# A projection chunk of the hybrid trunk kernel: products with high weight halves first, then those with low halves

## The reference, cut to what matters

```
h    = rmsnorm(x, g_pre)
proj = einsum('bld,de->ble', h, w_in)      # even: 1024 x 5648, odd: 1024 x 4104
...                                        # gated MLP and SSD scan (even), forgetting attention (odd)
o    = einsum('ble,ed->bld', y, w_out)     # even: 2048 x 1024, odd: 1024 x 1024
x    = x + rmsnorm(o, g_post)
```

## Time and profile before

| | us |
|---|---|
| median of 3 runs | 1733.57 |
| lowest and highest | 1732.59, 1736.33 |
| span of the profiled execution | 1733.1 |
| PE busy in it | 1618.7 (93%) |
| DVE, ACT, POOL busy | 820.3, 639.0, 431.9 |
| granted TensorE clock, mean | 0.973 |

### The profile page before, as it was taken

One profiled execution on the slowest core, in us unless ns is written; L12 is line 12 of the kernel. 1 busy time (PEld: TensorE's weight loads), 2 busy tenths in 40 slices (PEclk: granted clock), 3 DMA queues, 4 the chain that ended last, 5 costly groups with the idle time before them and its releaser, 6 DMA issues.

```text
span 1733.1 us, 27903 instructions
## 1 busy us (share of the span) xinstructions
PE 1618.7 (93%) x10174; PEld 1529.1 (88%) x10174; DVE 820.3 (47%) x1738; ACT 639.0 (37%) x1146; POOL 431.9 (25%) x261
## 2 busy tenths in 40 slices
PE   5899999998998999899997899999999999997995
PEld 4899999988998999799995788889888888986894
DVE  5745776674883122711117833443434344344426
ACT  6433332332224222511123344444444444444213
POOL 1113443451212121512211321211212121124113
PEclk9999999999999999899998999999999999998997
DMA  4121222112102111111140235523232332201103
GB/s 140 39 64 55 67 82 67 54 42 78 45 19 61 37 42 43 37 37 48 46 120 9 37 64 49 68 43 67 42 65 49 46 67 43 67 31 50 32 18 100
DMA packets 150349, 93.97 MB, mean 54 GB/s; under 512 B 8994, under 2 KB 144836, under 8 KB 150300
## 3 DMA queue, kind: packets, MB, share of 16 engines
q1 hardware_dynamic: 150300, 93.30, 23.5%
HBM read 78.95 MB, written 14.34 MB: 54 GB/s over the span
## 4 chain that ended last, share of the span: by engine, by line
PE 77%; DVE 8%; ACT 6%; issue 5%; POOL 1%; DMA 1%; SPq 0%; POOLq 0%; ACTq 0%; DVEq 0%
PE PB L639 72%; PE PB L643 5%; DVE NRML L1462 2%; DVE HX L1469 1%; ACT HH L1086 1%; ACT L1092 1%; DVE HL L1462 1%; ACT SB L1418 1%; DVE O L1462 1%; DMA XS<-in_x_prompt_dram 1%; ACT L1349 1%; ACT NRMH L1086 0%; DMA nf_rows<-NFROW 0%; DVE O L1469 0%; POOL HL L617 0%
## 5 line engine op out<-in xcount | busy, mean ns | idle before, releaser
L639 PE MATMUL PB<-HH,WH 128*128 128x352 f32 x2256 | 752.0, 333 | 36.3 <-DVE HL L1462 11.5
L639 PE MATMUL PB<-HH,WL 128*128 128x352 f32 x2256 | 731.9, 324 | 0.0
L639 PE MATMUL PB<-HL,WH 128*128 128x352 f32 x2256 | 731.5, 324 | 0.0
L639 PEld LDWEIGHTS PB<-HH,WH 128*128 128x128 f32 x2256 | 429.9, 191 | 60.2 <-issue 39.8
L519 POOL TENSOR_TENSOR WL<-WRAW,WH 128x1024 fp32r<-128x1024 f32 x102 | 249.4, 2446 | 771.1 <-ACT WH L1086 771.1
L639 PEld LDWEIGHTS PB<-HL,WH 128*128 128x128 f32 x2256 | 431.3, 191 | 0.0
L639 PEld LDWEIGHTS PB<-HH,WL 128*128 128x128 f32 x2256 | 430.0, 191 | 0.0
L1086 ACT ACTIVATE WH<-WRAW 128x1024 fp32r<-128x1024 f32 x102 | 107.4, 1054 | 90.0 <-PE PB L639 70.6
L1462 DVE TENSOR_TENSOR TMP<-O 128x352 f32 x48 | 25.2, 525 | 199.7 <-ACT O L1106 199.3
L1418 ACT ACTIVATE SB<-SB,small 128x128 f32<-128x128 f32 (+8 forms) x72 | 53.9, 748 | 81.7 <-DVE small L1466 81.6
L639 PE MATMUL PB<-PT,VTOK 128*128 128x128 f32 (+2 forms) x624 | 81.6, 274 | 0.1
(11 more groups left out here) (239 smaller groups left out, 2060.3 us busy)
## 6 DMA issues: line engine op xcount, KB each, us to landing
WRAW<-in_w_in_even_dram SPq DMA_DIRECT2D x44, 512.0 KB, 3.8
WRAW<-in_w_in_odd_dram SPq DMA_DIRECT2D x32, 512.0 KB, 8.4
ACSB<-acs_rows SPq DMA_DIRECT2D x16, 528.0 KB, 4.8
XS<-in_x_prompt_dram SPq DMA_DIRECT2D x16, 512.0 KB, 6.2
WRAW<-in_w_out_even_dram SPq DMA_DIRECT2D x16, 512.0 KB, 3.9
NFB<-nf_rows SPq DMA_DIRECT2D x8, 656.0 KB, 3.9
out_dram<-VTOK SPq DMA_DIRECT2D x8, 512.0 KB, 3.2
out_dram<-KTOK SPq DMA_DIRECT2D x8, 512.0 KB, 3.0
```

The lines of the kernel that those rows point to most:

```text
L639: return pe.matmul(out, lhsT, rhs, start=start, stop=stop)
```

## The change: what it does

Within a chunk the loop over the eight blocks issues only the two products with WH. A second loop behind it issues the eight products with WL. The first chunk of a tile waits on `w_high` at its start, and on `w_low` between the two loops. The waits on the low halves of the activations stay ahead of the two products of their block. The number of products, their operands and their bank are the same.

```diff
         def project_chunk(w, u, c, hi, lo, start=True, stop=True, ready=None, ks=range(KT)):
 
             if c == 0:
-                pe.wait_ge(S("w_low"), times(w, 1, 1))
+                pe.wait_ge(S("w_high"), times(w, 1, 1))
...
-                wh, wl = WH[:, slot(w), k, :], WL[:, slot(w), k, :]
+                wh = WH[:, slot(w), k, :]
                 mm(PB[c][:, 0:CH], wh, hi[:, k, cols], start=start and k == 0, stop=False)
                 mm(PB[c][:, 0:CH], wh, lo[:, k, cols], start=False, stop=False)
-                last = mm(PB[c][:, 0:CH], wl, hi[:, k, cols], start=False, stop=stop and k == KT - 1)
+            if c == 0:
+                pe.wait_ge(S("w_low"), times(w, 1, 1))
+            for k in ks:
+                last = mm(PB[c][:, 0:CH], WL[:, slot(w), k, :], hi[:, k, cols], start=False,
+                          stop=stop and k == KT - 1)
             if ks[-1] == KT - 1:
                 last.then_inc(S("p_chunk"), 1)
```

## The result

The changed kernel takes 1741.91 us (median of four runs, 1740.2 to 1743.92), the kernel before beside it 1734.04 (four runs). The ratio is 1.0046, with an interval of 1.0034 to 1.0058: slower by 7.9 us, outside the range of the prediction (1728.5 to 1740.5) and on the side to which it gave 0.24.

What follows compares the result with a forecast made beforehand. The prediction took PE's own product stream to be the bound. A -2.3, B -0.8, C +0.2 and +2.6, rate 0 and wait 0 summed to -0.3 us from 1733.57, giving 1733.3 us; range 1728.5 to 1740.5.

Steps and rivals of the forecast that it cites:

- A: Tile start at 524 us: PE starts 0.74 us earlier and avoids a 1.5 us low-clock cost; -2.3 us, other end -0.7.
- B: Forget gates' tile and next, 944 to 977 us: later last products against idle and low clock avoided; -0.8, ends -2.5, +0.9.
- C: Two tiles at 711 to 738 us with late low halves: losses of +0.2 (0 to +0.6) and +2.6 (other end +1.1).
- The added wait: Wait on w_low in the middle of about 100 first chunks: already met, so 0 us.
- The rate: Steps of 7,344 products, 0.1590 us apart: same count of each kind, so 0 us; bounds +6.8 and -2.8 us.
- Rival 2: Steps from WL to WL within chunks are slow: +6.8 us, 1740.4 us; chance 0.07.
- Rival 1: The wait in the middle of first chunks holds back weight loads: 11 us slower, 1744.6 us; chance 0.10.
- Rival 3: The new order runs faster throughout: 1 ns per product saves 7.3 us, 1726.0 us, full size 1661; chance 0.12.
- Rival 4: PE no earlier at A and B because other waits end last; sparse places still lose: 1737.5 us; chance 0.07.
- The 0.62 on no change: Whole kernel: chance that the measured time differs by no more than 0.2%, 3.5 us; faster 0.14, slower 0.24.

Runs made afterwards that it cites:

- the wait alone: Kernel before, old product order, but first chunks wait on w_high at their start and on w_low ahead of their third product: 1731.91 us, ratio 0.9991.
- the alternated weights: Kernel before, each block's products reordered to high by high, high input by low weights, low input by high weights: 1734.33 us, ratio 1.0005.
- three passes: Kernel before, each chunk run as eight high by high, eight low input by high weights, eight high input by low weights: 1751.01 us, ratio 1.0102.
- the moving block 0: Every product streams input block 0 (wrong sums): in the changed kernel 1741.6 us, ratio 1.004; in three passes 1744.25 us, ratio 1.0057.
- the paired blocks: Block order 0, 4, 1, 5, 2, 6, 3, 7 where input is complete: kernel before 1738.21 us, changed kernel 1740.21, old order with split wait 1736.33.
- The aligned version: Three passes with each block's input stretch shifted to begin at the same place within 512 bytes (wrong columns): 1743.75 us, ratio 1.0064.
- The version with two new chunks: Kernel before, with new order and weaker wait only in the first chunks of the tiles at 524 and 971 us: 1731.2 us, ratio 0.9984.
- order alone: Kernel before with the new order in every chunk, but first chunks still wait on w_low at their start: 1744.8 us, ratio 1.0065.

## Why the prediction was wrong

**A was right, its second half with luck**: -2.3 forecast, -2.2 in the trace. The start came 0.68 us earlier (0.74 forecast), the bank's read is the releaser, and the low stretch is gone. But in six of the ten versions with the weaker wait a low stretch of the same 3.4 us stands some 30 us behind A instead; the changed kernel happens to have neither (see the last section).

**B was right in its sum, by other parts**: -0.8 forecast, -1.1 found. The ten products at the lower clock took 3.10 us, as at the worse end, and the start is 0.18 us later (forecast: 1.0 earlier to 0.3 later). The other half of that end, a clock that stays low as long afterwards, did not come, so the middle was near because one half went either way.

**C was right**: +2.8 forecast (0.2 and 2.6), +2.7 found. The piece for the YB tile is within 0.1 us of nothing, since DVE's twelve and the difference behind them are as before. The YAL tile's is 2.1 for the later chunk, seven products at the lower clock, and 0.6 for the later rise.

**The added wait was right**: 0, by the run of the wait alone and by the step of 0.16 us at 528.50.

**The rate is the step that failed.** I put "The new chunk has the same count of each" kind of step and "By this it costs 0". The counts are right, and the conclusion isn't: it measured 1.01 ns per step, 7.6 us, nearly three times the largest other term. The 3 ns by which I told the kinds apart were not theirs. Means over a fixed order of three can't tell kind from position; the alternated weights show that the lengths stay at the position when the kinds are swapped. The single steps of the kernel before could have warned me: in the six-step pattern above one and the same kind, lo to hi, takes 162 and 155 ns in turn. Read to the ns, all rows of the stretch give the kinds 160.7, 158.5 and 158.0 ns where the prediction has 160.9, 158.5 and 157.7, so its bounds should have been +5.7 and -2.3 us. They had the same fault besides, since they took the nearest kinds as the ends, though the recorded +6.8 nearly held it. The right question would have been what else is periodic in the order: with three products per block the moving place changes 7 times in the 23 steps of a chunk, in the change 15 times, in three passes 23 times, and the three warm steps (159.3, 160.35, 161.3) grow with it. This count is a description of these three orders, not a law, as the moving block 0 and the paired blocks show.

**Rival 2** (WL behind WL slow, +6.8 us, 1740.4) has the right sign and nearly the right size for another reason. The steps within the low pass take 161.0 ns, 1.7 more than the mean before, but those of the high pass take 160.2, 0.85 more, and there are twice as many: the loss is half in each. **Rival 1** falls with the run of the wait alone. **Rival 3** falls; the 12 ns above 352 columns at 2.4 GHz do hang on the order, but of the six other orders that compute the same, one costs as much and five cost more. **Rival 4** gave the losses where the work is sparse, but A and B were gained. The Trainium skill's formula (TensorE: Matmul & The Clock Gate, "Back-to-back issue gap") has no term for where the operands lie, and the page gives it for isolated products, without room for weight loads. It gives 149.2 ns for 352 columns, and the warm chunks of these runs, which have a load for every product, lie between 158.2 and 166.7 (both with block 0). So the 72 us and the 1661 that the prediction worked out from it belong to another case than this stream.

The 0.62 on no change came from the four terms that were worked out from waits. The rate stood on 7,344 products, so an error of 0.5 ns in it, 3.7 us, was worth as much as the ends of all those terms together (-3.7 and +3.4), and a slower rate deserved more than the 0.07 of rival 2.

## What to carry to other kernels

Where an engine runs thousands of like instructions without a gap, price a reordering by its rate first, and take the length of a step from one trace only where position and kind are not locked to each other. Keep the order that the stream has and make the weaker wait by itself: the split wait gave some 1.6 us with the old order, and the new order in the two chunks that really stood behind a late arrival gave 2.6. In chunks fed by sparse arrivals keep together all that one arrival allows, since what is put off stands behind the last one.

## What was not expected of the hardware

**The place of the moving input sets the step.** With weights loaded for every product of 352 columns, at a granted clock of 1.00, the warm step was 159.3 to 161.4 ns by the order in which places within 512 bytes follow each other, and unchanged when all weights came from one block. The Trainium skill says that within the engines' side of SBUF PE, ACT and one pair of DVE's ports "never wait on anyone" (SBUF — State Buffer, "SBUF: two separate sides"). Nothing here shows another engine in PE's way, since the patterns repeat to the nanosecond from chunk to chunk of the output projection; its pace changes with the place it reads all the same.

**One place has several paces.** With block 0 throughout, column range 1 ran at 158.4 ns a step in the output projection, while the same range between attention products ran at 166.7 (steps of 166, 167 and 167 ns to its end):

```profile
1207.59 1.50 PE L639 MATMUL PB<-HL,WH 128*128 128x352 f32 x8
1208.92 1.49 PE L639 MATMUL PB<-HH,WL 128*128 128x352 f32 x8
1210.25 0.83 PE L639 MATMUL PB<-PT,VTOK 128*128 128x128 f32 x6
```

Eight products are 1.33 us here and 1.27 above, from 790.01 to 791.28, at the same granted clock. The aligned version has eleven such chunks. Ranges 0 and 2 vary as well: in 64 of their 192 warm chunks with block 0 in three passes the mean step is 161.0 to 161.5 and not 160.0. Each chunk keeps its pace from its first few steps to its end, so it looks as if the way in which a chunk is entered picks the pattern; this was not tried. The periods have a common measure: 160.0 and 166.7 for one step, 633.3 and 646.7 for four, and 953.3 for six fit the measured means (160.0, 166.7, 158.3, 161.6, 158.9 ns a step) within 0.1 ns, and all are whole multiples of 6.67 ns, which is 16 periods of 2.4 GHz (24, 25, 95, 97 and 143 times). So the stream seems locked to something that comes round every 6.67 ns, or a whole fraction of it. What that is stays open.

**A low stretch can move.** The version with two new chunks lost the one at A and got one at 553.8 which the kernel before did not have. Over all eighteen traces there are the stretch at A alone (only in the kernel before), the one near 555 alone (ten), both (three) and neither (four, the changed kernel among them). The idle time at A does not settle it: behind 1.57 us or less the clock never fell at A (ten versions), but with 1.88 us it fell (order alone) and with 2.22 it did not (weights alternated). So the shorter wait may well keep the clock up at A, but the 1.5 us that this gives are often lost again 30 us later, and why is not shown.

A gain counted on a stretch of low clock is safe only where the whole program shows fewer of them. Counted from 28 us on, where all three records have begun, the low stretches of the version with two new chunks come to 92.8 us, those of the kernel before to 96.4, of the changed kernel to 114.6. Of the 18 us that the changed kernel has more, 10 lie at B, where PE mostly waits, and what they cost is in the terms above.
